# A three-layer transformer kernel: softmax rows scaled in place and turned by transposes, and value products of two heads issued in alternation

## The reference, cut to what matters

```python
# first layer: stick-breaking attention, one head, one block of 128 queries
z = q_blk @ k.T * scale
log_not = where(mask, log_sigmoid(-z), 0.0)                 # mask: key before query
suffix = cumsum(log_not, reverse=True) - log_not
weights = where(mask, exp(log_sigmoid(z) + suffix), 0.0)
out = weights @ v

# third layer: three windows with strides 1, 4 and 16, joined by their log-sum-exp
for window, dil in DILATED_PATTERNS:
    o, lse = banded_causal_attention(split(q), split(k), split(v), window // dil)
w = softmax(stack(lses), axis=0)
o_a = einsum('pbhs,pbhsd->bhsd', w, stack(outs))
```

## Time and profile before

| | us |
|---|---|
| median of 3 runs | 3996.78 |
| lowest and highest | 3992.57, 3997.54 |
| the profiled execution's own time | 3995.06 |
| its span | 3993.0 |
| TensorE matmuls busy in it | 3699.0 (93%) |
| VectorE, ScalarE, GpSimd busy | 2177.2, 983.4, 407.4 |
| first attention, scores of the first part to the last `values` | about 109 to 422 |
| dilated attention | about 2991 to 3497 |

### The profile page before, as it was taken

The page is one execution under the profiler, slowest core; times in us unless marked ns, Lnnn a source line. Parts: engine busy times, 40 slices in busy tenths (PEclk is TensorE's granted clock), DMA queues, the critical chain, the costliest instruction groups (busy, mean ns, idle before and its releaser), DMA issues. The chain is left out here.

```text
span 3993.0 us, 43865 instructions
## 1 busy us (share of the span) xinstructions
PE 3699.0 (93%) x17499; PEld 2942.4 (74%) x17499; DVE 2177.2 (55%) x2929; ACT 983.4 (25%) x1986; POOL 407.4 (10%) x172
## 2 busy tenths in 40 slices
PE   7998899999998979976879999996999999989999
PEld 6664677888887658766758888885777777867587
DVE  6666476555666646989564444446223333346394
ACT  1566230000003331144220000004012223232362
POOL 0113022322320001523000000000000000000000
PEclk9998999999999989998989999997999999989999
DMA  4100222223222121020021111113111212143122
GB/s 157 32 22 22 74 83 89 77 77 114 77 101 75 43 81 48 22 74 17 22 85 42 42 47 58 42 63 117 40 37 70 77 56 72 46 182 101 57 59 79
DMA packets 137388, 267.59 MB, mean 67 GB/s; under 512 B 11680, under 2 KB 42516, under 8 KB 137236
## 3 DMA queue, kind: packets, MB, share of 16 engines
q1 hardware_dynamic: 137236, 265.50, 18.7%
HBM read 220.39 MB, written 45.09 MB: 66 GB/s over the span
## 5 line engine op out<-in xcount | busy, mean ns | idle before, releaser
L130 PE MATMUL banks<-region_parts 128*128 128x512 f32 x3226 | 1286.5, 399 | 88.0 <-DVE weight_chunks_parts L124 65.1
L132 PE MATMUL banks<-region_parts,weight_chunks_parts 128*128 128x512 f32 x2112 | 828.3, 392 | 0.0
L131 PE MATMUL banks<-weight_chunks_parts,region_parts 128*128 128x512 f32 x1984 | 779.2, 393 | 0.0
L130 PEld LDWEIGHTS banks<-region_parts 128*128 128x128 f32 x3226 | 612.4, 190 | 221.1 <-DVE weight_chunks_parts L124 44.9
L131 PE MATMUL banks<-region_parts 128*128 128x512 f32 x1658 | 649.9, 392 | 0.0
L132 PE MATMUL banks<-region_parts 128*128 128x512 f32 x1568 | 615.6, 393 | 0.0
L132 PEld LDWEIGHTS banks<-region_parts,weight_chunks_parts 128*128 128x128 f32 x2112 | 399.9, 189 | 85.3
L131 PEld LDWEIGHTS banks<-weight_chunks_parts,region_parts 128*128 128x128 f32 x1984 | 377.3, 190 | 81.1 <-issue 4.4
L618 ACT ACTIVATE region<-constants 128x512 f32<-128x512 f32 x128 | 81.1, 634 | 1260.8 <-DVE constants L550 1260.8
L131 PEld LDWEIGHTS banks<-region_parts 128*128 128x128 f32 x1658 | 314.4, 190 | 65.5 <-issue 2.7
L560 DVE TENSOR_TENSOR region<-region,banks 128x512 f32<-128x512 f32 x256 | 171.5, 684 | 323.1 <-PE banks L132 317.2
(11 more groups left out here) (387 smaller groups left out, 4865.3 us busy)
## 6 DMA issues: line engine op xcount, KB each, us to landing
weight_chunks<-in_w_in SPq DMA_DIRECT2D x19, 2048.0 KB, 8.1
weight_chunks<-in_w_up SPq DMA_DIRECT2D x16, 2048.0 KB, 8.4
weight_chunks<-in_w_down SPq DMA_DIRECT2D x16, 2048.0 KB, 7.7
extra<-in_w_ada SPq DMA_DIRECT2D x16, 1536.0 KB, 11.0
x_spill<-region SPq DMA_DIRECT2D x32, 512.0 KB, 10.9
weight_chunks<-in_w_out SPq DMA_DIRECT2D x8, 2048.0 KB, 8.4
region<-x_spill SPq DMA_DIRECT2D x32, 512.0 KB, 6.1
f_spill<-region SPq DMA_DIRECT2D x64, 256.0 KB, 2.0
```

The costliest lines, as they stand in the source:

```text
L130: pe.matmul(out, m.parts(lhs[0]), m.parts(rhs[0]), start=first, stop=False)
L131: pe.matmul(out, m.parts(lhs[0]), m.parts(rhs[1]), start=False, stop=False)
L132: return pe.matmul(out, m.parts(lhs[1]), m.parts(rhs[0]), start=False, stop=last)
```

## The change

It has two parts that are independent.

In the dilated attention `scale` no longer makes a diagonal matrix. It multiplies the unit's rows of weights in `SB` in place by the reciprocal of their sum, on VectorE, over all `t + 1` blocks. `turn` becomes a TensorE transpose with the identity. The wait of `scale` for the turns of unit `n - 2`, which kept the diagonal matrix from being overwritten, goes; `logits(n)` already has that wait.

In the first attention `values` runs at even steps only and does both heads of the pair: for each block of keys one product of the even head and one of the odd head. It waits for the copies of both parts. The number of products is as before.

```diff
@@ dilated_attention
-    diag = [m.cst[:, 3 + b, :] for b in range(2)]
...
             def turn(n, g):
                 h, t = units[n]
                 if g == 0:
-                    pe.wait_ge(diag_ready, n + 1)
+                    pe.wait_ge(scaled, n + 1)
                     if n >= 1:
                         pe.wait_ge(copied, turns[n - 1])
                 else:
                     pe.wait_ge(copied, turns[n] - 1)
                 for j in range(4 * g, min(t + 1, 4 * g + 4)):
-                    mm = pe.matmul(m.bank[:, TURN_BANK, (j % 4) * P:(j % 4 + 1) * P],
-                                   SB[n % 2][:, j * P:(j + 1) * P], diag[n % 2], start=True, stop=True)
+                    mm = pe.transpose(m.bank[:, TURN_BANK, (j % 4) * P:(j % 4 + 1) * P],
+                                      SB[n % 2][:, j * P:(j + 1) * P], m.ident)
                 mm.then_inc(turned, 1)
...
             def scale(n):
-                x = st[:, n % 3]
+                x, p = st[:, n % 3], SB[n % 2][:, 0:(units[n][1] + 1) * P]
                 dve.wait_ge(exp_ready, n + 1)
-                if n >= 2:
-                    dve.wait_ge(turned, turns[n - 2])
                 m.dve_link(dve, dve.reciprocal(x[:, 3:4], x[:, 2:3]))
-                dve.tensor_scalar(diag[n % 2], m.ident, x[:, 3:4], None, ALU.mult).then_inc(diag_ready, 1)
+                dve.tensor_scalar(p, p, x[:, 3:4], None, ALU.mult).then_inc(scaled, 1)
@@ embed_attention_1
             def values(i):
                 n, c, gi, t, odd, w, at, top = where(i)
-                h, b = 2 * groups[gi][0] + odd, 64 * odd
-                pe.wait_ge(s.copied, i + 1)
+                pe.wait_ge(s.copied, i + 2)
                 if gi >= 2 and i == last_part[gi - 1] + 1:
                     pe.wait_ge(s.rs_ready, gi - 1)
                 for j in range(w // P):
-                    mm = pe.matmul(m.bank[b:b + 64, 6 + gi % 2, (t % 4) * P:(t % 4 + 1) * P], v[:, 4 * c + j, h * 64:(h + 1) * 64],
-                                   aT[i % 2][:, j * P:(j + 1) * P], start=(top and j == 0), stop=(c == 0 and j == w // P - 1),
-                                   skip_group_check=True)
-                mm.then_inc(s.av_done, 1)
+                    for b in range(2):
+                        h = 2 * groups[gi][0] + b
+                        mm = pe.matmul(m.bank[64 * b:64 * b + 64, 6 + gi % 2, (t % 4) * P:(t % 4 + 1) * P],
+                                       v[:, 4 * c + j, h * 64:(h + 1) * 64], aT[b][:, j * P:(j + 1) * P],
+                                       start=(top and j == 0), stop=(c == 0 and j == w // P - 1), skip_group_check=True)
+                        if j == w // P - 1:
+                            mm.then_inc(s.av_done, 1)
...
+                if i >= 4 and i % 2 == 0:
+                    values(i - 4)
                 if i >= 4:
-                    values(i - 4)
```

More of the change, by code:

```diff
@@ L1610, in dilated_attention @@
     N = len(units)
-    tab, s_done, max_ready, exp_ready, diag_ready, turned, copied, o_done, y_ready = (
-        m.sem(f"da_{x}") for x in ("table_in", "scores", "max", "exp", "diag", "turned", "copied", "out_done", "out"))
+    tab, s_done, max_ready, exp_ready, scaled, turned, copied, o_done, y_ready = (
+        m.sem(f"da_{x}") for x in ("table_in", "scores", "max", "exp", "scaled", "turned", "copied", "out_done", "out"))
     F.w_high_ready, F.w_split, staged, m.stage_out = (
```

## The result

The changed kernel takes 3938.34 us (median of four runs, 3937.20 to 3943.05), the kernel before 3996.28 on the same chip (four runs, 3992.57 to 3997.54). The ratio is 0.9859, with a 95% interval of 0.9842 to 0.9876: 56 us faster by the ratio, 58 by the medians. The forecast was 3931, with a range of 3919 to 3947. The profiled execution took 3937.2 us (span 3935.2), 57.9 less than the profiled execution of before, where the sum of the prediction was 65.9. So 8 us of the sum are missing, and most of what follows is about these.

A forecast was written before the change was run, and what follows sets the result against it. TensorE was taken to bound the dilated attention and the first attention up to about 340 us. Savings of 31.7 + 30.2 + 4 = 65.9 us from 3995.1 make 3929.2, forecast as 3931 us, range 3919 to 3947 for 8 in 10.

The forecast's parts named there:

- the sum of the prediction: Whole program: 31.7 from dilated attention, 30.2 from first attention with filler and 4 from its last pairs, 65.9 us.
- Dilated attention: TensorE's turns: one pass less for each of 288 blocks at 0.11 us, 31.7 us saved.
- VectorE's added work: Dilated attention: wider scaling adds 15 us on VectorE, covered because the turn comes 10.5 us later; cost nothing.
- First attention with filler: First 34 pairs, 100 blocks: joining the heads saves one values group per pair, 30.2 us.
- The fixed part of a group: First attention: each values group costs 0.24 us besides 0.22 per block, all saved once per pair.
- rival 1: First attention paced by VectorE and ScalarE, half of 30.2 lost, 3946 us, chance 0.10; sign: new TensorE idle before turns naming VectorE.
- The last 14 pairs: End of the first attention, without filler, where TensorE waits for VectorE's weights: 4 us saved, between 0 and 13.
- 13.0: Last 14 pairs, 44 blocks: all that their removable values groups hold, 13.0 us; the most that could be saved there.
- It helps where the next scores start right behind an odd part's products: Last 14 pairs: where a shorter values group was to save time; a third was taken, 4 us.
- The likeliest case: Whole program: the forecast itself, 3931 us, chance 0.78, own range 3921 to 3939.
- Rivals 2, 3 and 5: 2: no head overlap, 3956, 0.03; 3: hidden chain holds dilated attention, 3963, 0.03; 5: transposes cost a quarter, 3915, 0.01.

The follow-up runs named there:

- Experiment 4: Changed kernel with a second in-place product, by 1.0, after each scaling of the dilated attention's weights; 3941.17 us, ratio 0.9863 to the kernel before.
- Experiment 7: Changed kernel with the joined value products a step later, in odd steps right ahead of the next scores; 3962.52 us, ratio 0.992 to the kernel before.
- Experiment 6: Changed kernel with VectorE's five-slice split of the last pair's weights cut into five steps; 3941.42 us, ratio 0.9863 to the kernel before.
- experiment 5: Changed kernel with one head per step again in the first attention from part 72 on; 3939.05 us, ratio 0.9859 to the kernel before.
- Experiment 8: Changed kernel without GpSimd's running sums of the pooling branch, whose output is then not computed; 3933.62 us, ratio 0.9846 to the kernel before.

## Why the prediction was right, and where its sum was off

**Dilated attention: 31.7 forecast, 34 measured.** TensorE's row is the limit, as the idle 3 us of 480 show, and a transpose costs what one pass costs. Nearly all of the 2.3 us come from the blocks whose turn stands beside products and scores, 0.128 a block and not 0.11; why a block saves more there was not tried. The factor of four for FP32 that the Trainium skill gives ("TensorE: Matmul & The Clock Gate", section "Terms") is not what these rows show: they have a factor of two. Nor is the clock that does not engage (same page, part on PE-mode transpose), with the transposes among other products: 1.00 in this stage.

**VectorE's added work: nothing, and nothing was measured.** Experiment 4 shows it with the work doubled.

**First attention with filler: 30.2 forecast, 23.7 measured** (24.3 at part 72, less 0.6 at the start). Two terms were mis-sized. The fixed part of a group was taken as 0.24 us, of which 0.10 was the start after an F pass. Of the two groups of a pair before, one stood ahead of a turn (the first in the earlier trace rows) and one right ahead of the next scores (the second), and I priced both as if all of it went. The second is gone, and the scores, which followed it at no extra cost, now pay the same 0.10 themselves. The saving is 0.13 + 0.22 per block: 34 pairs times 0.11 are 3.7 us. Experiment 7 saves the 0.10 by letting scores and products share the start, and at that place it costs far more than it brings. The second term is the loss by new waits, which the prediction put at nothing there: 2.6 us (4.0 us idle in the stretch in place of 1.4), of which 1.3 are the turns at 232.05 and 238.62 that name VectorE, 0.7 a sum of squares and 0.5 the wait for both copies, which the prediction had as costing nothing. The two turns are the sign that was to speak for rival 1, in a tenth of its size. Experiment 6 takes their waits away and gets 1.4 us back.

**The last 14 pairs: 4 forecast, 1.05 measured, of 13.0.** The step "It helps where the next scores start right behind an odd part's products" and the third taken for it failed; the sentence before it, that a shorter group mostly makes the wait longer, is what happened. TensorE was busy for 64.0 us of this stretch before (337 to 422) and is for 52.2 now (312.5 to 397), and idle for 21.0 before and 32.3 now. Single heads with a wait of their own do not do better (experiment 5). What the prediction did not look at is GpSimd. Its last group of sums and what follows lie beside the start of this quarter, before and after the change alike, and hold a good part of VectorE's scans and products, for which TensorE waits. Experiment 8 takes the sums away and the quarter gives 9.2 us in place of 1.05. That is probably for the most part not the 13.0 come true, since VectorE was held about as long in the kernel before (19.9 us against 21.0); what the change would be worth without the sums is not shown, as the kernel before was not run without them.

Together: 2.3 - 3.7 - 2.6 - 3.0 is -7.0; the stretches outside the change, 0.6 + 3.1 - 2.5 - 2, give another -0.8, and 0.2 is rounding. The likeliest case came true, and the time lies at the slow end of its range, 3921 to 3939. Some of that is luck: the first attention fell 9.4 us short, and 2.3 of it are hidden by a dilated stage that gave more than its term. Rivals 2, 3 and 5 are excluded by 0.055 us a pass, by 34 us in the stage, and by 0.112 to 0.128 a block.

## What to carry to other kernels

When a group of small matmuls is taken out, look at what will stand in its place: the extra cost of leaving the big passes may pass to the next group in line. A wait that appears with a change may stand where another stood; take it away before believing its size. Where an engine already waits, a shorter group on it is not time gained: look at its idle time as well as at its busy time. And where one engine waits for VectorE's products of two operands, look at what GpSimd does at that moment before shortening anything else.

## What the runs showed that was not expected

- Matmuls on the two halves of the columns overlap without being neighbours: with four passes of one head still ahead, the other head's passes started 0.055 us apart in between, and 16 passes took 1.52 us, against 1.03 alternated and 2.04 apart.
- A VectorE product of 128 columns took 0.29 us alone and 1.80 to 1.95 beside GpSimd's sums, ending just behind the GpSimd instruction that was under way; one of 512 columns took 2.67 in place of 0.69.
- The start after an F pass costs 0.10 us extra for a group on half of the rows or columns (64\*128, 128\*64), once per group, and nothing for a transpose of 128\*128 (0.24 in place of 0.23). The earlier trace rows show it only for the 128\*64 group, since the scores there stand behind another such group and pay nothing.
